# VectorE takes the expert slots in twos: two dots, then two diagonals

## The reference

```python
u_sel = expert_u[idx]                                  # 8 heads x 16 experts, rows of 1024
act = gelu(einsum('phkd,pd->phk', u_sel, xb))          # one dot of 1024 per expert and token
coef = softmax(best_s) * act
y = einsum('phk,phkd->pd', coef, expert_v[idx])        # sum of 128 rows of 1024, weighted
```

## Time and profile before

| | us |
|---|---|
| median of 3 runs | 1790.79 (1789.38 to 1791.67) |
| profiled execution, its own time | 1790.01 |
| its span, first to last instruction | 1788.2 |
| TensorE busy | 1573.0 |
| VectorE busy | 1497.8 |
| GpSimd busy | 807.5 |
| indirect DMAs of the experts | 512, landing 14.5 after issue at the median |

### The profile page before, as it was taken

One profiled execution on the slowest core, in us unless ns is written; L12 is line 12 of the kernel. 1 busy time (PEld: TensorE's weight loads), 2 busy tenths in 40 slices (PEclk: granted clock), 3 DMA queues, 4 the chain that ended last, 5 costly groups with the idle time before them and its releaser, 6 DMA issues.

```text
span 1788.2 us, 19181 instructions
## 1 busy us (share of the span) xinstructions
PE 1573.0 (88%) x4808; PEld 814.3 (46%) x4808; DVE 1497.8 (84%) x3520; ACT 351.8 (20%) x971; POOL 807.5 (45%) x554
## 2 busy tenths in 40 slices
PE   7999999999999878888888888888888888888887
PEld 6888878777534333333333333333333333333332
DVE  5788977677689988888888888888888888888887
ACT  5222423546110211110101010110011112001101
POOL 2000000000045456665566666556666665566662
PEclk9999999999999999999999999999999999999999
DMA  6565562331299999999999999999999999999996
GB/s 237 193 228 181 208 258 85 124 141 60 98 417 421 421 421 421 421 418 405 422 422 422 421 421 422 422 421 423 422 421 422 422 422 422 422 422 422 422 422 288
DMA packets 92835, 620.72 MB, mean 347 GB/s; under 512 B 11360, under 2 KB 11376, under 8 KB 23408
## 3 DMA queue, kind: packets, MB, share of 16 engines
q0 software_dynamic: 77936, 566.81, 76.8%
q1 hardware_dynamic: 14848, 53.26, 8.3%
HBM read 617.94 MB, written 2.10 MB: 347 GB/s over the span
## 4 chain that ended last, share of the span: by engine, by line
DMA 40%; PE 30%; DVE 14%; issue 7%; DVEq 5%; POOL 3%; ACT 1%; POOLq 0%; SPq 0%; ACTq 0%
DMA arena<-in_experts,idx 39%; PE ps L439 7%; PE ps L440 7%; PE ps L441 7%; DVE arena L1453 7%; PE ps L665 7%; POOL arena L428 3%; DVE arena L1480 2%; DVEq L1305 2%; PE ps L575 1%; DMA arena<-in_w_in 1%; DVEq L1347 1%; DVE lnw L1325 1%; DVEq L1323 1%; DVEq L1381 0%
## 5 line engine op out<-in xcount | busy, mean ns | idle before, releaser
L665 PE MATMUL ps<-arena 128*128 128x512 f32 x2048 | 1001.6, 617 | 196.8 <-DVE arena L1480 192.3
L428 POOL DMA_INDIRECT arena<-in_experts,idx x512 | 784.3, 1532 | 656.0 <-PE ps L665 342.7
L665 PEld LDWEIGHTS ps<-arena 128*128 128x128 f32 x2048 | 354.9, 190 | 794.4 <-DVE arena L1480 525.1
L1453 DVE CUSTOM_DVE_ANT_0 arena<-arena,ada 128x1024 f32<-128x1024 f32 x448 | 548.5, 1224 | 74.8 <-DMA arena<-in_experts,idx 72.7
L917 ACT ACTIVATE lnw<-lnw 128x1 f32<-128x1 f32 x512 | 103.9, 203 | 1123.7 <-DVE lnw L1453 1123.7
L1480 DVE TENSOR_SCALAR arena<-ident,lnw 128x128 f32<-128x128 f32 x512 | 171.1, 334 | 2.6 <-ACT lnw L917 0.9
L391 POOL DMA_DIRECT2D arena<-in_w_ada x24 | 12.7, 530 | 222.6 <-DVE ada L1020 218.0
L1020 DVE SCALAR_TENSOR_TENSOR ada<-arena,cact,ada 128x512 f32<-128x512 f32 x96 | 72.1, 751 | 16.8 <-DMA arena<-in_w_ada 9.8
L439 PE MATMUL ps<-xT_hl,w_hl 128*128 128x512 f32 x192 | 75.6, 394 | 9.2 <-DVE xT_hl L986 9.2
L981 DVE TENSOR_TENSOR w_hl<-arena,w_hl 128x1024 fp32r<-128x1024 f32 x47 | 57.4, 1221 | 27.0 <-ACT w_hl L703 27.0
L1453 DVE CUSTOM_DVE_ANT_0 arena<-arena 128x1024 f32<-128x1024 f32 x64 | 78.1, 1220 | 2.3 <-DMA arena<-in_experts,idx 1.8
(11 more groups left out here) (251 smaller groups left out, 1652.2 us busy)
## 6 DMA issues: line engine op xcount, KB each, us to landing
arena<-in_w_ada POOLq DMA_DIRECT2D x24, 1024.0 KB, 5.5
arena<-in_w_in SPq DMA_DIRECT2D x44, 512.0 KB, 3.4
arena<-in_experts,idx POOLq DMA_INDIRECT x512, 14.5
arena<-in_w_out SPq DMA_DIRECT2D x14, 512.0 KB, 5.4
lnw<-in_w_in SPq DMA_DIRECT2D x8, 512.0 KB, 4.0
arena<-in_w_grp POOLq DMA_DIRECT2D x4, 1024.0 KB, 8.1
arena<-in_w_out SPq DMA_DIRECT2D x1, 4096.0 KB, 13.4
arena<-in_w_q SPq DMA_DIRECT2D x1, 4096.0 KB, 12.8
```

What stands on the lines that cost most here:

```text
L428: nc.gpsimd.indirect_dma_start(slot(n), None, experts, bass.IndirectOffsetOnAxis(ap=idx[:, e, n:n + 1], axis=0)).then_inc(arr[n % RING], 16)
L665: last = mm(ps[half][:, :], lhsT=diag[:, n % RING, :], rhs=slot(n)[:, DM + half * T:DM + (half + 1) * T], start=(e == 0 and n == 0), stop= ...
L1453: nc.vector.tensor_tensor_reduce(out=urow, in0=urow, in1=rows, scale=1.0, scalar=0.0, op0=ALU.mult, op1=ALU.add, accum_out=dots[:, e, n:n ...
```

## The change

The wait for the Gelu and the diagonal no longer stand in every slot. In an even slot VectorE does the dot and the pieces only. In an odd slot it does the dot and the pieces, and then the two diagonals, that of the even slot first, each behind its own wait. The same instructions are issued as before. The other engines' programs are unchanged.

```diff
                         if late and (step, n) in late_h2:
                             h2_piece(*late_h2[step, n])
-                        dve.wait_ge(gelu_done, step * TOPK + n + 1)
-                        ts(diag[:, n % RING, :], ident[:, :], acts[:, e, n:n + 1], gate[:, e, n:n + 1],
-                           ALU.mult, ALU.mult).then_inc(diag_ready, 1)
+                        if n % 2:
+                            for m in (n - 1, n):
+                                dve.wait_ge(gelu_done, step * TOPK + m + 1)
+                                ts(diag[:, m % RING, :], ident[:, :], acts[:, e, m:m + 1], gate[:, e, m:m + 1],
+                                   ALU.mult, ALU.mult).then_inc(diag_ready, 1)
```

## The result

The changed kernel takes 1794.14 us (median of 15 runs, 1791.45 to 1799.29), the kernel before 1790.69 (15 runs, 1789.33 to 1792.27): ratio 1.0022, 95% interval 1.0015 to 1.0029, 3.45 us more by the medians, 2.7 to 5.2 by the interval. The runs also scatter more. The profiled execution of the changed kernel took 1798.12 us, 4 us above its median.

The account below looks back on a forecast made before the run. The prediction took the expert transfers from HBM as the bound. Its terms, 0 + 0 + 0.7 + 0 + 1.8 = +2.5 us, gave 1792.5 from the profiled 1790.01 or 1793.3 from the median; forecast 1793.0, range 1790 to 1798.

Parts of the forecast that it names:

- The bound: Expert stage: VectorE and TensorE both wait for the expert transfers from HBM, 2.48 us per slot at 422 GB/s.
- (a): VectorE's own time: no instruction is removed and it idles before arrivals anyway; 0, with -2.2 us as the bound.
- (b): Steady stage: even slots released some 2.5 us later, odd ones 1.8 to 2.0; landing falls to about 12 us, cost 0.
- (c): Start of the expert stage: later refills thin the queue to about one transfer for some 15 us; 0.7 us.
- (d): Three boundaries between tiles: refills go out later but 7.7 us ahead, above 5.7; cost 0, upper bound 6.6 us.
- (e): Tail after the last row pair lands: TensorE has two slots to do instead of one; +1.8 us.
- The sum: Whole kernel: 0 + 0 + 0.7 + 0 + 1.8 = +2.5 us.
- The dry queue: Rival: queue runs dry at refills after the start and tile boundaries; 10.5 us and the tail, 1803; chance 0.14.
- The clock in mid-stage: Rival: TensorE's clock falls in each pair's gap, making TensorE the bound; about 520 us more, 2310 us; chance 0.02.

## Why the prediction was right, point by point

- **The bound** held. The dots stand 2.48 us apart before and after, and the rate in mid-stage is 422 GB/s in both.
- **(a) VectorE, 0**: right, shown by the run in which only TensorE changed (3.3 us over, the changed kernel 3.45), as far as medians with 1.6 us to either side can show it.
- **(b) Later release, 0 in mid-stage**: right. Landing 12.3 us where about 12 was forecast; pairs in mid-tile alone cost nothing that can be told (1.0001).
- **(c) The start, 0.7**: right. The issues came where the working put them (508.23, 509.94, 513.45 and 515.16, with a first issue 0.7 us later in this execution). The window 500 to 560 shows 417 instead of 422 GB/s, 0.7 us. The dots lag 0.7 us at dot 64, and as much where only TensorE changed, though one execution of each cannot carry a tenth: with pairs at the edges it was 0.3. The estimate from the page "DMA: Bandwidth & Descriptors" of the Trainium skill (section "Anatomy of one DMA"), 4.4 us for a lone transfer, would have put this term at 0. The trace does not bear the 4.4 us out: the first transfer of the stage landed 5.7 us after the start of its issue in the kernel before, 5.5 in the changed one, and 5.5 to 6.2 in the other runs whose traces have it.
- **(d) The boundaries, 0**: this is the step that failed, in size and not in place. The idle stretch (3.32 us for 3.2) and the shortest landing (7.7 us for 7.7) were right. Wrong was the floor to which they were compared: 5.7 us, the landing of one transfer into an empty queue. A stream needs more in reserve: rates fell where the shortest landing was 6.6 to 7.7 us (401 and 405 GB/s), and the three boundaries cost 1.1 us in the median execution of the run in which only TensorE changed, 4.8 in the changed kernel's profiled one, 4 us above its median. But no single floor comes out of the traces. A median landing of 9.4 to 9.7 us went with 420 GB/s in the second tile and 409 in the first, 7.9 us at the shortest with 422 and with 417, and the kernel before dropped to 347 at 10.7. A thin queue makes a loss possible; where it falls changes from execution to execution. Slots 0 and 1 also took 6.73 us at the falling clock instead of 5.61.
- **(e) The tail, 1.8**: 1.71 us measured, alone in its place in every kernel whose last two slots are a warm pair.
- **The sum**: 2.5 forecast, 3.45 measured. The tail explains 1.7; some 1.7 remain for start and boundaries, where 0.7 stood, and the median execution of the run in which only TensorE changed splits it into 0.7 and 1.1. The term that was mis-sized is that of the boundaries: forecast 0, measured 1.1 us.
- **The rivals.** The dry queue was the right mechanism at a sixth of its price. The gaps in the DMA share that were its sign are there in small: 0.95 and 0.94 in two stretches of 5 us, 1155 to 1160 and 1165 to 1170, behind the second boundary. The clock in mid-stage did not fall (1.00 from 1000 to 1120), with idle stretches of 1.0 to 1.5 us; but it was a real neighbour: singles ahead of a pair, or fours, brought the idle stretch to 3.1 us and more, and the clock fell. The page "TensorE: Matmul & The Clock Gate" of the Trainium skill (section "Why this matters for your kernels") warns against idle stretches between bursts of matmuls. The trace agrees in the main: a pair takes 3.70 us at the full clock and took 5.1 to 6.8 behind most idle stretches of 3.0 to 3.5 us, but in the run with singles ahead of pairs it stayed at 3.70 behind five of them.

Open is why the window behind the first tile boundary is weak in the kernel before too (352 and 347 GB/s with a landing time of 10.7 us), and not in the run with pairs in mid-tile (422 from 820 to 880, before 410). Nor is it known why the first tile loses more than the others when the queue is shallower. No run took these places apart.

## What to carry to other kernels

When the transfers set the beat, a rearrangement of engine work is worth what it does to the release of buffers: cover in mid-stage can be ample while the edges, where the queue is already thin, pay. That a shortened landing time is still above that of a lone transfer is no proof that it costs nothing; even a landing time once seen at full rate is no guarantee, so compare the time from the first issue to the last use, beside a run with the depth alone changed. Grouping work into bursts also groups the idle time between them, and in the tail the whole last burst stands uncovered.

## What was not expected of the hardware

The loss is steep. One slot less in flight cost 1.0 us (within its uncertainty; its landing time was not recorded), two (landing 9.7 us) 12.8 us, and pairs with one slot less (9.8 us) 13.4 us, although the first transfer of the stage lands in 5.5 to 6.2 us. In the thin stretches the rate drops to 401 to 405 GB/s over 50 or 60 us while the DMA share still reads 1.00, so the share hardly shows such a loss; the rate does. And a change of rhythm directly ahead of a tile's end can cost more than the rhythm itself: 36 pairs at the tiles' edges (four tiles by nine; the expectation had miscounted them) cost 8.6 us, 256 pairs everywhere 3.3. The same change at the start of step 1 cost nothing.
